# Two-layer hybrid encoder trunk with a hierarchical mixture of experts: the first set of experts by row chunks, the first gather in two parts, two parts of one load earlier, softmax by head halves

## What is computed

```python
def hierarchical_moe(h, norm_g, w_group, b_group, w_router, b_router, w_gate_up, w_down):
    xt = rms_norm(h, norm_g).reshape(B * S, D)
    g_idx = jnp.argmax(softmax(xt @ w_group + b_group))          # 4 groups
    top_p, top_i = lax.top_k(softmax(e_logits of that group), 2)  # 8 experts each
    gates = one_hot(expert_id) * (g_w * top_p)
    for w_gu (1024 x 1024), w_d (512 x 1024), g in 32 experts:
        a, b = jnp.split(xt @ w_gu, 2, axis=-1)
        acc = acc + ((silu(a) * b) @ w_d) * g[:, None]

def reference(x, positions, ...):
    h = x + conformer_conv_module(x, ...)     # rms norm, 1024->2048, GLU, 31 taps, layer norm, silu, 1024->1024
    h = h + hierarchical_moe(h, ...)
    k, v = shared_mla_kv(h, ...)
    h = h + mla_attention_layer(h, k, v, ...) # scores, chunk mask, softmax, p @ v, output weights w_o
    h = h + hierarchical_moe(h, ...)
```

## Time and profile before

| | |
|---|---|
| median of 3 runs | 1118.01 us (1117.9 to 1118.22) |
| profiled execution | 1118.59 us, of which the span of its trace is 1116.9 us |
| busy share of the span | PE 90%, PE weight load 39%, DVE 21%, ACT 16%, POOL 5% |
| DMA | 430.73 MB, mean 386 GB/s |
| mean granted TensorE clock | 0.983 of 2.4 GHz |

### The profile page before, as it was taken

One profiled execution on the slowest core, in us unless ns is written; L12 is line 12 of the kernel. 1 busy time (PEld: TensorE's weight loads), 2 busy tenths in 40 slices (PEclk: granted clock), 3 DMA queues, 4 the chain that ended last, 5 costly groups with the idle time before them and its releaser, 6 DMA issues.

```text
span 1116.9 us, 11486 instructions
## 1 busy us (share of the span) xinstructions
PE 1008.0 (90%) x4848; PEld 435.5 (39%) x4848; DVE 238.0 (21%) x525; ACT 173.5 (16%) x438; POOL 58.4 (5%) x92
## 2 busy tenths in 40 slices
PE   8999999989897989889799899999998979897887
PEld 7885532333232323223265554332323232232322
DVE  5993411201020100101035714201010101020101
ACT  4865300000000000000045513000000000000000
POOL 2890000000000000000000000000000000000000
PEclk9999999999999999999999999999999999999999
DMA  9794899999999999999996558999999999999997
GB/s 313 215 365 165 344 428 428 429 427 428 427 429 427 427 430 427 426 428 429 395 383 222 226 209 328 430 428 428 425 430 428 425 431 425 428 429 425 431 421 287
DMA packets 61073, 430.73 MB, mean 386 GB/s; under 512 B 12264, under 2 KB 22591, under 8 KB 38238
## 3 DMA queue, kind: packets, MB, share of 16 engines
q1 hardware_dynamic: 60894, 429.86, 93.8%
q10 hardware_dynamic: 126, 0.14, 0.0%
HBM read 428.94 MB, written 1.05 MB: 385 GB/s over the span
## 4 chain that ended last, share of the span: by engine, by line
PE 48%; DMA 40%; DVE 7%; SPq 4%; ACT 1%; issue 1%; DVEq 0%
DMA ring<-in_w_down_dram 25%; PE bank L941 15%; DMA zone<-in_w_down_dram 14%; PE bank L988 11%; PE bank L1026 6%; DVE bank L1324 4%; PE bank L930 3%; PE bank L1220 2%; PE bank L879 2%; SPq L446 2%; PE bank L1113 1%; PE bank L1135 1%; PE bank L1089 1%; PE bank L1097 1%; DMA pos_i<-in_positions_dram 1%; PE bank L997 1%
## 5 line engine op out<-in xcount | busy, mean ns | idle before, releaser
L941 PE MATMUL bank<-ring,zone 128*32 128x512 f32 x1152 | 337.0, 612 | 39.2 <-DMA ring<-in_w_gate_up_dram 26.8
L941 PE MATMUL bank<-zone 128*32 128x512 f32 x872 | 276.4, 608 | 25.6 <-DMA zone<-in_w_gate_up_dram 13.9
L988 PE MATMUL bank<-ring,xT 128*32 128x512 f32 x592 | 161.8, 593 | 13.0 <-DMA ring<-in_w_down_dram 6.8
L941 PEld LDWEIGHTS bank<-ring,zone 128*32 128x32 f32 x1152 | 87.8, 113 | 219.2 <-issue 218.9
L941 PEld LDWEIGHTS bank<-zone 128*32 128x32 f32 x872 | 70.7, 112 | 145.7 <-issue 145.4
L1447 DVE TENSOR_TENSOR xT<-xT,bank 128x512 f32<-128x512 f32 x16 | 11.0, 687 | 459.6 <-PE bank L941 459.6
L988 PE MATMUL bank<-zone,xT 128*32 128x512 f32 x304 | 103.9, 593 | 4.9 <-DMA ring<-in_w_down_dram 2.0
L1452 DVE TENSOR_TENSOR h<-bank,h 128x512 f32<-128x512 f32 x64 | 44.2, 691 | 266.6 <-PE bank L1026 266.6
L682 ACT ACTIVATE xT<-bank 128x512 f32<-128x512 f32 x16 | 9.6, 597 | 539.5 <-PE bank L941 539.5
L988 PEld LDWEIGHTS bank<-ring,xT 128*32 128x32 f32 x592 | 42.2, 110 | 94.8 <-issue 88.5
L1026 PE MATMUL bank<-zone,xT 128*128 128x512 f32 x128 | 63.1, 615 | 1.8 <-ACT zone L692 1.6
(11 more groups left out here) (264 smaller groups left out, 649.8 us busy)
## 6 DMA issues: line engine op xcount, KB each, us to landing
ring<-in_w_gate_up_dram SPq DMA_DIRECT2D x72, 2048.0 KB, 35.1
zone<-in_w_gate_up_dram SPq DMA_DIRECT2D x54, 2048.0 KB, 33.6
ring<-in_w_down_dram SPq DMA_DIRECT2D x40, 2048.0 KB, 35.7
zone<-in_w_down_dram SPq DMA_DIRECT2D x20, 2048.0 KB, 37.0
ring<-in_a_pw_w_dram SPq DMA_DIRECT2D x8, 1024.0 KB, 12.2
ring<-in_w_down_dram SPq DMA_DIRECT2D x8, 1024.0 KB, 17.7
ring<-in_a_pw_w_dram SPq DMA_DIRECT2D x2, 2048.0 KB, 11.4
ring<-in_w_o_dram SPq DMA_DIRECT2D x2, 2048.0 KB, 21.0
```

The source lines that it names most:

```text
L941: ins = nc.tensor.matmul(bank[b][s * CAP:(s + 1) * CAP, :], xs[:, k, s * CAP:(s + 1) * CAP], rhs[s][:, b * HALF:(b + 1) * HALF], start=(k ...
L988: ins = nc.tensor.matmul(bank[2 + b][s * CAP:(s + 1) * CAP, :], hidT[:, k, s * CAP:(s + 1) * CAP], units[s][:, k, b * HALF:(b + 1) * HALF] ...
```

## The change

1. **All of set 0 by row chunks.** `by_blocks` is true only for n other than 0. `gate_up` takes units 4 to 7 one at a time as well, and a new `down_first` does units 8 to 11 row by row.
2. **First gather in two parts.** k = 0 to 4 before the first chunk of `gate_up`, k = 5 to 7 behind it.
3. **Two parts of unit 3 early.** Parts 2 and 3 (`y_sb`, `spare`) are issued before the wait for the logits: in layer 0 after unit 6, in layer 1 after unit 9. For this the router weights of layer 0 move from `spare` into `zone`, with a wait of SP for a transpose of PE (`cols_tr`) ahead of the small loads.
4. **Softmax of t = 0 by even and odd heads**: maximum, exponentials, division, transposes and products with the values in halves; PE waits for `smax_ready` 3 (bank 7 read) before the second half of the `w_o` products of t = 0. ACT loads the table of Sqrt before it waits for the last outputs of the heads.
5. **Scatter of the last set**: token tile 0 before the last half unit, tile 1 behind it.
6. **Start**: 6 idle matmuls in place of 14; the fourth block of `xT` is scaled by DVE and no longer by ACT.

```diff
-        wr = [spare[:, SP0:SP0 + KD * NR].rearrange("p (k r) -> p k r", r=NR), sb("wr1", [P, KD, NR])]
-        SP1 = SP0 + KD * NR
+        wr1 = sb("wr1", [P, KD, NR])
+        SP1 = SP0
...
+        wr = [zone[:, moe0:moe0 + KD * NR].rearrange("p (k r) -> p k r", r=NR), wr1]
...
         def by_blocks(n, u):
-            return n != 0 or u >= 4
+            return n != 0
...
+            sp.wait_ge(cols_tr, 2)
             for l in range(L):
                 sp.dma_start(wr[l][:, :, NE:NR], a["w_group"][l].rearrange("(k p) g -> p k g", p=P)).then_inc(small2_in, 16)
...
                     if g == APART:
+                        if l == 1:
+                            parts_apart(1, (2, 3))
                         sp.wait_ge(logits_done, 2 * l + 2)
-                        for s in range(SIDE):
+                        parts_apart(l, (0, 1))
...
                 if g == 7:
+                    sp.wait_ge(hb_ready, 2)
+                    parts_apart(0, (2, 3))
                     sp.wait_ge(pw2_done, 3)
...
+                if t == 1:
+                    nc.scalar.activation(warm[:, :], eps_c[:, :], ACT.Sqrt)
                 act.wait_ge(o_done, 2 * t + 2)
...
-            for _ in range(14):
+            for _ in range(6):
                 nc.tensor.matmul(bank[7][:, 0:P], ident[:, :], ones[:, :], start=True, stop=True)
...
-                        if first and half == 0:
-                            for k in range(4):
+                        if first:
+                            for k in range(4 * half, 4 * half + 4):
                                 unit = landed(k)
                                 sides = unit if k == APART else [unit[:, s, :] for s in range(SIDE)]
                                 chunk(sides, k, range(SIDE)).then_inc(e["used"], 1)
+                                if k == 0:
+                                    gather(n, range(5, KD))
                             continue
...
+                def down_first(n, landed):
+                    pe.wait_ge(e["hidT_ready"], n + 1)
+                    for k in range(KF):
+                        unit = landed(GU + k)
+                        ins = down_rows(k, 0, unit)
+                        if k == KF - 1:
+                            ins.then_inc(e["half_done"], 1)
+                        down_rows(k, 1, unit).then_inc(e["used"], 1)
...
                     down_rows(KF - 2, 1, landed(UNITS - 2)).then_inc(e["used"], 1)
-                    scatter(n, 0)
+                    scatter(n, 0, tiles=(0,))
                     down_rows(KF - 1, 1, landed(UNITS - 1)).then_inc(e["used"], 1)
+                    scatter(n, 0, tiles=(1,))
                     scatter(n, 1)
...
                 pe.wait_ge(xn_ready, 2 * l + 4)
-                gather(0)
+                gather(0, range(0, 5))
...
                 for hf in range(2):
-                    for hh in range(H):
+                    if t == 0 and hf == 1:
+                        pe.wait_ge(smax_ready, 3)
+                    for hh in EVEN_ODD:
...
-            for b in (0, 2):
+            for b in (0, 2, 3):
                 across(0, b, "a_norm_g")
...
-            masked(0)
+            link(masked(0))
+            max_of_half(0)
             link(masked(1))
-            minus_max(0)
-            for n in range(2, 5):
-                masked(n)
-            probs(0)
-            link(masked(5))
+            max_of_half(1)
+            masked(2)
+            probs_of_half(0)
+            masked(3)
+            probs_of_half(1)
             probs_across(0)
-            minus_max(1)
+            masked(4)
             heads_out(0)
-            probs(1)
+            link(masked(5))
+            minus_max(smax[:, 1, :], sc1)
+            probs(ssum[:, 1, :], sinv[:, 1, :], sc1, S, 2 * H)
             add_attention(0)
```

109 lines of the change are left out of this document (63 added, 46 removed).

## The result

The changed kernel takes **1111.17 us** in the median of 4 runs (1110.95 to 1111.55). The kernel before took 1117.95 us in the same comparison (4 runs). The ratio is 0.9934, with a 95% interval of 0.9922 to 0.9947. The prediction was 1111.8 us, with a range of 1109.8 to 1115.2.

The account below looks back on a forecast made before the run. Each layer's experts were taken as bound by the DMA stream of weights. Terms -1.3 - 1.5 + 0.8 - 2.9 - 0.4 - 0.7 - 0.2 = -6.2 us took 1118.59 to 1112.4 (median 1111.8), range 1109.8 to 1115.2.

Parts of the forecast that it names:

- restart layer 0, with rows: Weight stream restarting at unit 10's issue in layer 0: sooner issue and shorter queue gain 1.5 us, less the 4 KB rows' cost.
- restart layer 1, with rows: Weight stream restarting at unit 10's issue in layer 1: split gather gains 1.3 us, early parts nothing, less the rows' cost.
- softmax: Attention's softmax of t = 0 by halves: the w_o products start 2.9 us sooner, bounds 0 and 3.5.
- Sqrt table: Table load moved into ACT's wait before layer 1's router: 0.4 us gained, not 1.3, since logits are needed too.
- end of layer 1: Last scatter's 0.78 us wait for ACT's copy gets covered by the scatter of tile 1: 0.7 us gained.
- end of layer 0: One scatter tile less ahead of the last half unit, which lands about when PE begins it: 0.2 us gained.
- start: Shorter warm-up and DVE scaling the fourth block: nothing gained, as DVE's first GLU follows its own work on the positions.
- as if begun at 136.7, then at 135.2: When layer 0's stream effectively restarts at full rate, before and after the change: gain 1.5 us, not 1.3 + 2.45.
- The row chunks: Set 0 in 4 KB rows: PE's saving worth nothing, slower transfer of units 10 and 11 costs 0.2 us each, +0.8 in all.
- Rival 1: Units 10 and 11 load at 260 GB/s as four experts' rows: +12.6 us in place of +0.8, 1123.6 us; chance 5%.
- its rival: Softmax halves give nothing because DVE, with more and shorter steps, becomes the chain: 1114.7 us; chance 12%.
- Rival 3: With 6 idle matmuls at the start, the convolution's first matmuls run at 1.2 GHz, everything 4.4 us later: 1116.2 us; chance 4%.

Follow-up runs that it names:

- the candidate: Changed kernel with the first gather cut after column 0, which is scaled alone, columns 2 to 7 behind the first chunk: 1112.74 us, repeated 1111.96.
- the blocks: Changed kernel with first-set units 4 to 11 as blocks again: 1111.56 us, ratio 0.9933; with only down units 8 to 11 as blocks: 1111.24, ratio 0.9928.

## Why the prediction was right

The time from one trace to the other, step by step (us):

| step | forecast | measured | by |
|---|---|---|---|
| restart layer 0, with rows | -1.5 + 0.4 | -1.50 | both stages, 429.71 to 428.21 |
| restart layer 1, with rows | -1.3 + 0.4 | -1.16 | 429.46 to 428.30 |
| softmax | -2.9 | -2.88 | 13.10 to 10.22; undone, 13.04 |
| Sqrt table | -0.4 | -0.43 | 0.44 to 0.01; undone, 0.43 |
| end of layer 1 | -0.7 | -0.91 | 13.32 to 12.41 |
| end of layer 0 | -0.2 | +0.03 | 11.03 to 11.06 |
| start | 0 | -0.83 | first GLU 21.73 to 20.90 |
| sum | -6.2 | -7.68 | spans 1116.87 to 1109.20 |

- **The restarts** were right in mechanism, and in size with both edits in place. The queue of layer 0 now ends just ahead of the release, and the reckoning "as if begun at 136.7, then at 135.2" gave 1.5 us, which is what was found. "Not 1.3 + 2.45" says that the gains don't add up, but not that each edit needs the other: the experiments gave -0.3 for the early parts and +0.7 for the split alone, and the late parts missed their expectation. The rule "an issue that comes x us earlier ends the layer x us earlier" held for this step and not for the next one: the candidate's 1.36 us gave -0.9 to +1.1 per layer.
- **The row chunks** were mis-sized: +0.8 was forecast for units 10 and 11, and nothing was found. The step that failed is that of 417 against 427 GB/s, from which 0.2 us a unit was taken: the rate of a stretch of the convolution, which has its own gaps, was taken as the rate of the row format. The Trainium skill's line rate from 512 B on ("DMA: Bandwidth & Descriptors", Specifications), with which I didn't go, fits the measurement: the 4 KB rows cost 0.1 us in one layer and -0.1 in the other. Its fall to 103 GB/s for rows 4 MiB apart (same page, Latency and other measured facts) doesn't show: the gate-and-up row chunks, whose four experts lie so, have the 417 GB/s of the earlier trace rows. The page's figure is for copies from HBM to HBM with that distance between the 128 rows, which no run here has. Units 10 and 11, for which the rival was priced, don't bear on it: they are down units, whose experts lie 2 MiB apart. Rival 1 is refuted by their 358 and 356 GB/s in the 10 us from the release, pause included, and by the blocks, which were no faster. Its 260 GB/s has its like in the changed kernel (271 GB/s from 598 to 605, in the attention); what holds the rate down there wasn't tried.
- **The softmax** came as worked out to 0.02 us, and its rival (nothing, because DVE's order eats it) fell with the version that undoes it.
- **The ends.** The 0.7 of layer 1 was read from a trace in which PE's clock was at half, and at half clock it is right (0.7). At full clock it is 0.16. The changed kernel's trace has both at once, order and clock, so 0.91. That this lies near the forecast is luck: at least 0.2 of it, and by the full-clock price 0.75, is the clock that stayed up, which nothing in the prediction or the change accounts for. In layer 0 the forecast 0.2 didn't come: PE there waits 0.62 us for the last half unit, and work taken from ahead of a landing brings nothing.
- **The start** is scatter: 21.73 in one trace of before and 21.04 in the other. That would account for most of the difference between the 7.6 us of the profiles and the 6.8 of the medians. Rival 3 was right that the first matmuls run slower with 6 idle ones, by 1.2 us in the transposes, and wrong about what it costs: the first GLU isn't later. That the clock is the reason isn't shown, since the granted clock reads 1.00 there.

So the forecast of 1111.8 was 0.6 above the median, mainly since the rows' 0.8 didn't come.

## What to carry to other kernels

Where a stream of transfers bounds a kernel, ask when its queue runs empty and when its next release comes: of two edits that move one each, a single one may bring next to nothing, and only both together shorten the pause. Read the price of a wait at the end of a kernel together with PE's granted clock in those microseconds, since an edit that saves 0.7 us at half clock saved 0.16 at full clock. And take terms under half a microsecond from stages between two fixed instructions, not from medians, which scatter by more.

## What was unexpected

- **The stream has laggards.** The sixteen completion events of one transfer end 0.4 to 2.6 us apart at the first transfer behind the release of layer 0 and 3.3 to 5.1 us apart at the 81st, and the layer ends with the last. In the changed kernel the first event of the 81st transfer came 3.5 us ahead of the last in each layer, so about 7 us in all lie in this drift, about as much as the whole change brought; how much of it could be won wasn't tried. Each pair of slow packets (1.1 us in place of 0.61, some 30 us apart) begins with a packet that loads instructions.
- **A pause levels them.** With the queue empty at the restart the spread was 0.4 to 1.0 us in layer 0, without a pause 1.4 to 2.6; in layer 1 it was 0.4 to 1.7 and 1.8 to 2.2. Filling the pause is therefore worth less than its length: of 1.36 us per layer, 0.5 to 1.0 were left in the first events, and -0.9 to +1.1 in the length of the layer.
- **PE's clock fell to half in the last set** in five of fourteen traces, each time within 0.6 us of PE taking up work again behind a wait of 2.6 to 2.7 us for a landing, but six others had that wait too (2.65 to 2.73 us, the changed kernel 2.66) and kept the full clock. What decides it stays open.
